# Attention's weighted sums as three fp32r products, two groups behind the scores

## What is computed

```python
for layer in range(DEPTH):                       # DEPTH = 2, SEQ = 1024, N_META = 16, D_MODEL = 1024
    if layer < N_A_LAYERS:                       # 1
        h, v_first = rwkv7_layer(h, v_first, ...)        # RWKV-7 time mixing
        if layer == N_A_LAYERS - 1:
            k_sh, v_sh, c_all = shared_kv(h, ...)        # K, V, cumulative log forget gates
            h = h[:, N_META:]
    else:
        h = fox_layer(h, k_sh, v_sh, c_all, ...)
# fox_layer, for each of 16 heads of 64 channels and 1,024 queries over 1,040 keys:
logits = einsum(q, k) * scale + c[t] - c[s]      # causal
p = softmax(logits);  out = einsum(p, v)
return h + (out * silu(z)) @ w_out
```

## Time and profile before

| | us |
|---|---|
| median of 3 runs | 1925.34 (1925.02 to 1925.78) |
| the profiled execution | 1921.38 |
| its span, first to last instruction | 1919.6 |
| TensorE matmuls busy | 1836.2 (96%) |
| VectorE busy | 977.6 (51%) |
| ScalarE busy | 946.9 (49%) |
| GpSimd busy | 431.8 (22%) |

### The profile page before, as it was taken

How to read it: one execution, slowest core, us unless ns; L and a number is a source line. 1 busy time by engine, 2 the same in 40 slices (tenths; PEclk the granted TensorE clock), 3 DMA queues, 4 the chain that set the end, 5 groups by cost and what they waited for, 6 DMA issues and landing times.

```text
span 1919.6 us, 55790 instructions
## 1 busy us (share of the span) xinstructions
PE 1836.2 (96%) x24271; PEld 1596.3 (83%) x24271; DVE 977.6 (51%) x1873; ACT 946.9 (49%) x1712; POOL 431.8 (22%) x425
## 2 busy tenths in 40 slices
PE   6899999999999999999798999999999999999898
PEld 5798989898998989998698778888888888887676
DVE  7456665666666665666433652534344444344521
ACT  6455454545555554544323525364645555555621
POOL 2223142423323242421000321212121213111010
PEclk8999999999999999999799989999999999999899
DMA  6101010100101010101242110111111101111334
GB/s 234 45 11 45 6 52 9 45 16 28 31 19 42 6 52 9 52 9 30 85 147 103 46 34 16 35 29 28 29 28 29 38 24 39 28 29 28 99 100 136
DMA packets 103735, 89.85 MB, mean 47 GB/s; under 512 B 4101, under 2 KB 95864, under 8 KB 103240
## 3 DMA queue, kind: packets, MB, share of 16 engines
q1 hardware_dynamic: 99544, 66.41, 11.9%
q0 software_dynamic: 3168, 17.14, 2.8%
q10 hardware_dynamic: 784, 2.76, 0.4%
HBM read 64.96 MB, written 21.33 MB: 45 GB/s over the span
## 4 chain that ended last, share of the span: by engine, by line
PE 88%; DVE 5%; ACT 3%; issue 2%; DMA 1%; POOL 0%; SPq 0%; DVEq 0%; ACTq 0%; POOLq 0%
PE ps L1951 8%; PE ps L2563 7%; PE ps L1952 6%; PE ps L2460 6%; PE ps L1953 6%; PE ps L2461 6%; PE ps L2462 6%; PE ps L1877 3%; PE ps L2043 3%; PE ps L1879 3%; PE ps L1878 3%; PE ps L2062 3%; PE ps L2534 2%; PE ps L2506 2%; PE ps L2535 2%
## 5 line engine op out<-in xcount | busy, mean ns | idle before, releaser
L1951 PE MATMUL ps<-xh,wh 128*128 128x258 f32 (+1 forms) x1024 | 320.5, 313 | 4.1 <-ACT arena L1045 2.7
L1952 PE MATMUL ps<-xh,wl 128*128 128x258 f32 (+1 forms) x1024 | 291.6, 285 | 0.0
L1953 PE MATMUL ps<-xl,wh 128*128 128x258 f32 (+1 forms) x1024 | 291.1, 284 | 0.0
L2460 PE MATMUL ps<-xh,wh 128*128 128x348 f32 x744 | 254.5, 342 | 3.3 <-ACT arena_b L1305 3.3
L2461 PE MATMUL ps<-xh,wl 128*128 128x348 f32 x744 | 240.1, 323 | 0.0
L2462 PE MATMUL ps<-xl,wh 128*128 128x348 f32 x744 | 239.8, 322 | 0.0
L1822 DVE TENSOR_REDUCE arena_b<-ps 128x1 f32<-128x144 f32 (+4 forms) x224 | 106.2, 506 | 205.6 <-PE ps L2510 171.7
L1951 PEld LDWEIGHTS ps<-xh,wh 128*128 128x128 f32 x1024 | 193.8, 189 | 16.7 <-ACT arena L1045 4.6
L1952 PEld LDWEIGHTS ps<-xh,wl 128*128 128x128 f32 x1024 | 194.5, 190 | 1.9
L1953 PEld LDWEIGHTS ps<-xl,wh 128*128 128x128 f32 x1024 | 193.6, 189 | 0.0
L1014 ACT ACTIVATE arena<-ps,pp 128x257 f32<-128x257 f32 (+1 forms) x128 | 61.3, 479 | 227.2 <-PE ps L1953 227.2
(11 more groups left out here) (298 smaller groups left out, 4476.6 us busy)
## 6 DMA issues: line engine op xcount, KB each, us to landing
wr<-in_w_in SPq DMA_DIRECT2D x33, 512.0 KB, 4.5
xt_scr<-arena POOLq DMA_DIRECT2D x2, 4176.0 KB, 13.0
wr<-in_kv_w SPq DMA_DIRECT2D x16, 512.0 KB, 4.0
wr<-in_b_w_in SPq DMA_DIRECT2D x16, 512.0 KB, 3.9
arena<-xt_scr SPq DMA_DIRECT2D x8, 522.0 KB, 4.6
arena<-oa_scr SPq DMA_DIRECT2D x8, 520.0 KB, 4.5
wr<-in_w_out SPq DMA_DIRECT2D x8, 512.0 KB, 5.2
ob_scr<-arena_b POOLq DMA_DIRECT2D x16, 256.0 KB, 2.9
```

Source lines behind the costliest of these rows:

```text
L1951: pe.matmul(bank, wh[:, j, k, :], xh[:, k, t], start=(k == 0), stop=False)
L1952: pe.matmul(bank, wl[:, j, k, :], xh[:, k, t], start=False, stop=False)
L1953: mm = pe.matmul(bank, wh[:, j, k, :], xl[:, k, t], start=False, stop=(k == KO - 1))
L2460: pe.matmul(bank[:, 0:SEG], wh[:, slot, k, :], xh[:, k, t], start=(k == 0), stop=False)
```

## The change

The weights P and V are each split into a high fp32r part and a low rest, and the product is Vh Ph + Vl Ph + Vh Pl. ScalarE rounds P (step `high`, by a copy from `pt`), GpSimd subtracts (step `low`); for V, ScalarE puts the transposed rows into `bsq`, then copies the high part, VectorE subtracts. P's parts are rings of four in spare slots of `wh` and `wl` (in the last head in stacking tiles). `pt` remains a ring of four fp32 tiles, two of them in the tile that held masks and levels. The weighted sums of g come behind scores g + 2, the last two groups' at the end of the round. The waits: an exponential waits for the low part four units back, a high part for the weighted sum four units back. GpSimd's list is now taken from the same steps: low parts of P by group, and between them scalings, low parts of weights, and stores with issue and wait apart. Semaphores of the forget gates are merged into two.

```diff
--- before.py
+++ after.py
@@ -253,12 +252,10 @@
         ident = sb("ident", [P, P])
         identb = sb("identb", [P, P], BF16)
-        identf = sb("identf", [P, CH])
         head_ones = sb("head_ones", [P, P])
         all_ones = sb("all_ones", [P, P])
-        ones_r = sb("ones_r", [P, P], F32R)
-        masks = sb("masks", [P, 4 * CH])
-        levels = sb("levels", [P, 6 * CH])
+        tables = sb("tables", [P, SEQ])
+        masks, levels, identf = tables[:, 0:4 * CH], tables[:, 4 * CH:10 * CH], tables[:, 10 * CH:11 * CH]
         causal = sb("causal", [P, 2 * P], BF16)
...
@@ -283,7 +280,9 @@
         qb2 = [sb(f"qb2{e}", [P, TP], F32R) for e in range(2)]
         qc2 = [sb(f"qc2{e}", [P, TP], F32R) for e in range(2)]
         EXTRA = slice(HD, HD + 3)
-        ARENA_B = 13848
+        VB = 3 * HD
+        vhi, vlo = (sb(n, [P, NT, VB], F32R) for n in ("vhi", "vlo"))
+        ARENA_B = 10412
         arena_b = sb("arena_b", [P, ARENA_B])
...
         kb, qb, zb, vb, bsq, brs, zg = (carve_b(TP) for _ in range(7))
-        vflat = [carve_b(NT * P).rearrange("p (t x) -> p t x", t=NT) for _ in range(2)]
-        pt = [carve_b(512) for _ in range(4)]
+        pt = [carve_b(512) for _ in range(2)] + [tables[:, 0:512], tables[:, 512:]]
...
+        v_rows = bsq[:, 0:NT * HD]
+
+        def v_cols(e):
+
+            return slice(2 * e * HD, (2 * e + 1) * HD)
+
+        p_store = [a[:, 2:4, :, :].rearrange("p s k c -> p (s k c)") for a in (wh, wl)]
+        p_last = ((ka[0], qa[0]), (kb2[0], qb2[0]))
+
+        def p_part(n_, low):
+
+            i = n_ % 4
+            if n_ // NU == 2 * KO - 1:
+                return p_last[low][i // 2][:, 512 * (i % 2):512 * (i % 2) + 512]
+            return p_store[low][:, 512 * i:512 * i + 512]
...
-            steps = [("scores", e, 0)]
+            steps = []
             for g in range(len(GROUPS)):
-                steps += fill[g]
-                if g + 1 < len(GROUPS):
-                    steps += [("scores", e, g + 1)]
-                steps += [("weighted", e, g)]
-            return steps
+                steps += [("scores", e, g), ("high", e, g)]
+                if g >= P_LAG:
+                    steps += [("weighted", e, g - P_LAG)]
+                k = 0
+                while k < min(2, len(fill[g])) and fill[g][k][0] == "smax":
+                    k += 1
+                steps += fill[g][:k] + [("low", e, g)] + fill[g][k:]
+            return steps + [("weighted", e, g) for g in range(len(GROUPS) - P_LAG, len(GROUPS))]
...
@@ -881,31 +898,61 @@
             scale_b(0, 3)
             scale_b(1, 0)
-            for p in range(KO - 1):
+            def issue_ob(p, e):
+
+                pool.wait_ge(S.o_gated, 2 * p + e + 2)
+                pool.dma_start(ob_scr[p][head(e), :], ob[head(e), :]).then_inc(S.ob_stored, 16)
+
+            def end_ob(p, e):
+
+                pool.wait_ge(S.ob_stored, 16 * (2 * p + e) + 16)
+                pool.sem_inc(S.ob_free, 1)
+
+            def round_attention(p, e, more):
+
                 n = N_B + 4 * (p + 1)
-                scale_b(p + 1, 1)
-                scale_b(p + 1, 2)
-                if p == 0:
-                    pool.wait_ge(S.w_lo, n + 2)
-                low_b(n + 1)
-                scale_b(p + 1, 3)
-                low_b(n + 2)
-                if p:
-                    store_ob(p - 1, 1)
-                if p + 2 < KO:
-                    scale_b(p + 2, 0)
-                else:
-                    pool.wait_ge(W_LOADED[N_BO % 2], 16 * (N_BO // 2 + 1))
-                    pool.wait_ge(S.w_scaled, 1 + 4 * KO)
-                    pool.sem_inc(S.w_scaled, 1)
-                low_b(n + 3)
-                store_ob(p, 0)
-                low_b(n + 4)
-            store_ob(KO - 2, 1)
-            store_ob(KO - 1, 0)
-            pool.wait_ge(S.w_lo, N_BO + 3)
-            low_b(N_BO + 2, 2)
-            low_b(N_BO + 3, 3)
+                for st_ in order(e, more):
+                    kind = st_[0]
+                    if kind == "low":
+                        g = st_[2]
+                        for w in GROUPS[g]:
+                            n_k, _, n_q, _, _ = unit(w)
+                            n_ = NU * (2 * p + e) + w
+                            pool.wait_ge(S.p_hi, n_ + 1)
+                            pool.tensor_tensor(p_part(n_, 1)[0:n_k, 0:n_q], pt[n_ % 4][0:n_k, 0:n_q],
+                                               f32(p_part(n_, 0)[0:n_k, 0:n_q]), ALU.subtract).then_inc(S.p_lo, 1)
+                        if e == 0 and g == 0 and more:
+                            scale_b(p + 1, 1)
+                            scale_b(p + 1, 2)
+                        elif e == 0 and g == 3 and more:
+                            scale_b(p + 1, 3)
+                        elif e == 0 and g == 7 and p:
+                            end_ob(p - 1, 1)
+                        elif e == 1 and g == 0 and more:
+                            if p + 2 < KO:
+                                scale_b(p + 2, 0)
+                            else:
+                                pool.wait_ge(W_LOADED[N_BO % 2], 16 * (N_BO // 2 + 1))
+                                pool.wait_ge(S.w_scaled, 1 + 4 * KO)
+                                pool.sem_inc(S.w_scaled, 1)
+                        elif e == 1 and g == 5:
+                            end_ob(p, 0)
+                    elif kind == "proj" and st_[2:] == (0, 0) and st_[1] < 3:
+                        if p == 0 and st_[1] == 0:
+                            pool.wait_ge(S.w_lo, n + 2)
+                        low_b(n + 1 + st_[1])
+                    elif kind == "wsplit" and more:
+                        low_b(n + 4)
+                    elif kind == "gated" and p >= st_[1]:
+                        issue_ob(p - st_[1], st_[1])
+                    elif kind == "bsplit":
...
                     act.wait_ge(S.b_done, chunk(p, L_SK) + 3)
+                if p >= 0:
+                    act.wait_ge(S.v_lo, 2 * p + 2)
...
@@ -1297,17 +1346,19 @@
                         e, i = st_[1:]
                         local = (L_VROW0, L_VROW1)[e] + i
                         act.wait_ge(S.b_done, chunk(p, local) + 1)
-                        if p + e > 0:
-                            act.wait_ge(S.pv_done, NU * (2 * p + 1 - e))
-                        c = slice(e * HD, (e + 1) * HD)
                         bank = ps[:, B_G[local % 2], :]
+                        rows_v = v_rows.rearrange("p (t c) -> p t c", c=HD)
                         if i == 0:
-                            act.activation(vflat[e][:, 0:7, c], bank[:, 0:7 * HD].rearrange("p (t c) -> p t c", c=HD),
+                            act.activation(rows_v[:, 0:7, :], bank[:, 0:7 * HD].rearrange("p (t c) -> p t c", c=HD),
                                            ACT.Copy).then_inc(S.b_evac, 1)
                         else:
-                            act.activation(vflat[e][:, 7, c], bank[:, 0:HD], ACT.Copy)
-                            act.activation(vflat[e][0:META, 8, c], bank[0:META, HD:2 * HD], ACT.Copy)\
+                            act.activation(rows_v[:, 7, :], bank[:, 0:HD], ACT.Copy)
+                            act.activation(rows_v[0:META, 8, :], bank[0:META, HD:2 * HD], ACT.Copy)\
                                 .then_inc(S.b_evac, 1)
+                            act.wait_ge(S.b_evac, chunk(p, local) + 1)
+                            if p + e > 0:
+                                act.wait_ge(S.pv_done, NU * (2 * p + 1 - e))
+                            act.activation(vhi[:, :, v_cols(e)], rows_v, ACT.Copy).then_inc(S.v_hi, 1)
                     elif kind == "gate":
                         act.wait_ge(S.o_gated, 2 * p + 1)
...
@@ -1326,9 +1377,19 @@
                             n_ = NU * (2 * p + e) + w
                             act.wait_ge(S.st_done, n_ + 1)
                             if n_ >= 4:
-                                act.wait_ge(S.pv_done, n_ - 3)
+                                act.wait_ge(S.p_lo, n_ - 3)
                             act.activation(pt[n_ % 4][0:n_k, 0:n_q], ps[0:n_k, B_ST[i], 0:n_q], ACT.Exp,
                                            scale=SCALE).then_inc(S.p_exp, 1)
+                    elif kind == "high":
+                        e, g = st_[1:]
+                        for w in GROUPS[g]:
+                            n_k, _, n_q, _, _ = unit(w)
+                            n_ = NU * (2 * p + e) + w
+                            act.wait_ge(S.p_exp, n_ + 1)
+                            if n_ >= 4:
+                                act.wait_ge(S.pv_done, n_ - 3)
+                            act.activation(p_part(n_, 0)[0:n_k, 0:n_q], pt[n_ % 4][0:n_k, 0:n_q], ACT.Copy)\
+                                .then_inc(S.p_hi, 1)
                     elif kind == "weighted":
...
@@ -1752,9 +1813,9 @@
             dve.wait_ge(S.x_lo, N_XL + 2 * KO)
             dve.wait_ge(S.proj_done, AFTER_A + N_F + 1)
             g = G[N_F % 2]
```

(26 more changed lines are left out.)

64 lines of the change are left out of this document (34 added, 30 removed).

## The result

The changed kernel takes 2006.16 us (median of 4 runs, 2005.34 to 2007.25) against 1925.18 us (1924.44 to 1925.78) for the kernel before on the same chip. The ratio is 1.0421, 95% interval 1.0403 to 1.0439. The prediction was 2003 us, with 0.84 for slower. The profiled execution has a span of 2003.5 us, 83.9 more than before's 1919.6.

A forecast was written before the change was run, and what follows sets the result against it. TensorE, busy 84.52 of 85 us in a full pair's window, was taken as the bound. Saving -19, waits +75, last pair +8 and clock +14 gave +78 on the median 1925.34, about 2003 us; range 1927 to 2050.

The forecast's parts named there:

- The saving: TensorE's weighted sums: three fp32r products in place of fp32 gain 1.2 us for each of 16 heads, -19 us.
- the walk: One pair followed on the trace's clock with each queue's new order: 10.65 us of TensorE waits a pair, +75 over seven.
- first row maxima, third stacking step: Even head's start: VectorE's stacking alternates with GpSimd's operations, so TensorE waits 3.4 us before the first maxima.
- second row maxima, first reduction: Even head: TensorE, after two maxima and half a projection, waits 2.3 us for VectorE's first reduction.
- odd head, 16-column scores: Odd head's start: ScalarE's added copies delay its last exponentials and weighted-sum cover is lost; TensorE waits 1.6 us.
- The clock: In the pairs, idling lowers TensorE's granted clock to half: between 0 and 28 us, the middle taken, +14.
- Rival (c): The clock falls in every pair and the last suffers more: +28 and growing waits, above 2050 us; chance 0.06.
- a sign named in advance: Windows of a full pair should show TensorE busy some 10 to 12% less of the time.
- The last pair: The eighth pair, without projections, gets the copies and loses cover at its start: +8 us, bounds 0 and 16.
- Rival (a): Shared-port waits don't come, ScalarE's do: 4.55 us a pair, +18, 1943 us; chance 0.20 for 1930 to 1960.
- Rival (b): ScalarE's copies are hidden, so the saving decides: not slower, 1906 us with no delay at all; chance 0.12.
- Edits costed at nothing: Renamed semaphores, masks and levels in one tile, constant tile, DVE memsets, GpSimd's split output stores: 0 us.

## Why the prediction was right

Its sign and its mechanism held. The size came out 3 us from the forecast in part by luck: terms were off in opposite directions, and the sum hides it.

**The saving**: -19 us, measured -15 by the product alone. The estimate from widths was 1.1 us a head, and 0.1 was added for a change between formats; 0.9 was had. The addition had no row behind it, and the shorter forms, scaled with 0.02 us fixed, had a part too, whose size was not taken apart.

**The waits**, us a pair, by the walk and as the mean of the six full pairs:

| place | walk | measured |
|---|---|---|
| V's bank, even head | 0.9 | 0.45 |
| first row maxima, third stacking step | 3.4 | 2.9 |
| second row maxima, first reduction | 2.3 | 0.45 (1.3 in two pairs, none in four) |
| sums of squares | 0.65 | 0.5 |
| row maxima 8, logarithm | 1.4 | 1.1 |
| odd head, 16-column scores | 1.6 | 1.6 |
| odd head, a group on | 0.4 | none |
| odd head, V's bank and a reduction, not named | | 0.55 |
| sum | 10.65 | 7.5, so 7.0 more than before's 0.5 |

Five of the seven named waits came in every full pair. The second largest came in two of six, and the smallest not at all. What came without a name is small, and 0.5 us was there before, at V's bank in the odd head. The walk through the alternation is good to half a microsecond. Its clock is that of before; the exponentials of the even head start 20.27 us later after than before (1340.39 for 1320.12). Shifted by that, the third step was to end at 1351.8 and ended at 1351.23, and TensorE was to ask for it at 1348.4 and did at 1348.41. The walk let the second step and the third each lose a turn to GpSimd, and in the trace both are long (2.40 and 1.25 us for 0.70).

The wait at the second row maxima was mis-sized by a thing that the walk held fixed: TensorE's own speed. It was to do half a projection in 1.9 us. At a granted clock of 0.50 it took about twice that, and arrived within 0.1 us of the end of the first reduction, which came 0.7 us earlier than walked. In the two full pairs that have the wait the clock fell some 2 us later. In all six the second row maxima start 16.3 us after the head's first scores: the reduction sets that time, and half clock ahead of it costs nothing. With the subtractions cut, the clock was up there, and the wait is 1.7 us in every full pair.

**The clock** was the term of the sum that was sized too small: +14 us, bounds 0 and 28, so 2 us a pair and 4 at most. The run with the scalings moved puts it at 4.2 a pair, some 25 us for the six full pairs. It was taken as the middle between nothing and the 9.8 us stretch of the last pair, with no ground for the middle; the like stretch was the better guide. Rival (c) had the clock at the measured size, but expected above 2050 us, because it let the waits grow, and they came out smaller. So a full pair was predicted at 10.65 - 2.4 + 2 = 10.25 us, and the 10.4 measured are 7.0 of waits, -1.9 of saving (TensorE's busy time alone), 4.2 of clock and a rest of 1.1. The rest is TensorE's busy time with the scalings moved, 88.6 us a pair, against the 87.5 that the product alone leaves. The prediction had no term for it. The order brings 0.65 of it, as the run of the order alone shows; a little is the one stretch at half clock, and the remainder is not taken apart.

For the same reason a sign named in advance came out differently: TensorE was to be busy 10 to 12% less in a full pair. It is busy 93.22 of 100.26 us, 93.0%, where it was 84.52 of 85, 99.4%. An engine at half clock counts as busy.

**The ends.** Pair 0 was counted as a full pair, 10.25 us, and cost 5.6: it held a long stretch at half clock before the change too (mean 0.94 before, 0.93 after), and its first wait for the stacking is 0.65 us, not 2.9. The last pair was to be worth +8, less its share of the saving 5.6; it is 10.6 to the end of the execution. Of these 3.8 us are idle time and 6.8 busy time, with the mean clock at 0.90 for 0.95: there the clock had not been costed at all. Its largest waits are 4.0 us for exponentials, 2.4 for VectorE and 1.5 for a low part of P, the one place where the slack of the low parts failed in the changed kernel. The two errors are of like size and cancel, which is luck.

**Rival (a)**, without the port's waits 1943 us, had 0.20. Its condition is nearly that of the run with the scalings moved, where a full pair has 3.7 us of waits more than before, for the 4.55 it gave. That run's 1958.73 us are 16 more. A full pair there is 2.9 us longer than before for 2.15 (less waiting, but 0.5 of saving not had and the rest of 1.1), some 6 us over the seven pairs. Another 8 lie in the last pair, which was to add 2.6 and is as long (165.0 us to the end) as in the changed kernel. **Rival (b)**, copies hidden, falls by the cuts: ScalarE's copies cost 2.3 us a pair, more than the 2.0 that the product saves, and even without them and without the subtractions the kernel is 28 us slower than before.

**Edits costed at nothing** (semaphores, tables in one tile, stores) show no wait of their own in the lists. GpSimd's split stores could not be seen to cost anything; no run undid them.

The parts of the 10.4 us a pair, each from a pair of runs that differ in it: product -2.0, order +1.4, place of the scalings +7.5 (in the full kernel), copies +2.3, subtractions +4.7. They add up to 13.9, more than 10.4, since the scalings' place and the subtractions share one cause: without copies and subtractions the place costs 3.5. Then the parts are -2.0 + 1.4 + 3.5 + 2.3 + 4.7 = 9.9, and the 0.5 that was left over above makes 10.4. That this sum closes proves nothing, as each part is a difference between neighbours in one row of runs.

## What to carry to other kernels

When one engine is busy throughout, work on the others is free only where its queue reaches it in time: walk the queues in order at the places where the busy engine asks, and take the cover that the change removes as a cost of its own. Here a cheaper product was worth 15 us, and the order that its operands needed took 14 back. When GpSimd and VectorE both read SBUF, place GpSimd's long operations where VectorE has nothing urgent: that was worth 47 us for an edit of two positions in a list. And cost a new stall together with the clock that follows it.

## What the runs showed of the hardware

VectorE's stacking steps and GpSimd's scalings and subtractions, which all read and write SBUF, take turns by whole instructions: VectorE's 64x1044 copy took 2.40 us in the shadow of a scaling and 0.70 with GpSimd idle. By the Trainium skill (SBUF — State Buffer, the section on the two separate sides) the port pair is locked for a whole instruction; the trace agrees, with both numbers above and with the two scalings, 5.27 us under VectorE's steps for 1.9 a piece undisturbed.

The clock was costed too low. A granted clock of 0.50 came with a wait of 2.88 us, and TensorE was busy all through the 8 us at 0.50 that followed. It also came where no wait was above 1.6 us, with one group's distance, where TensorE is idle 8.1 us a pair: the mean over the six full pairs is 0.95 (the same as in the changed kernel, with 7.5 us idle). With the subtractions cut, TensorE is idle 6.5 us a full pair with a longest wait of 1.7 us, and four of the six pairs stay at 1.00. With the scalings moved, 4.2 us a pair, the same waits at the same places gave full clock in five pairs and a stretch at 0.50 in one. Which pattern of waits brings the clock down is left open. No run here separates the length of a wait from its neighbours.
